# Turning the router's and the experts' operands by DMA instead of by the matrix engine

## What is computed

```
hn = rms_norm(h, ffn_norm_g)                       # per token
group = top1 of 4, experts = top2 of 8 in it       # router: hn @ [w_group_router | w_expert_router], 36 columns
for each 128-row block of rows sorted by expert e:
    a = silu(xb @ w_gate[e]) * (xb @ w_up[e])      # 128 x 512, xb = rows of hn, 128 x 1024
    y = (a @ w_down[e]) * gate                     # added to h at the token's row
```

## Time and profile before

| | us |
|---|---|
| median of 3 runs | 2934.15 (2933.95 to 2938.82) |
| the profiled execution | 2933.64 |
| its span, first to last instruction | 2932.0 |
| PE's first expert matmul | 1513.8 |
| mean granted clock of PE | 0.986 of 2.4 GHz |

### The profile page before, as it was taken

One profiled execution on the slowest core, in us unless ns is written; L12 is line 12 of the kernel. 1 busy time (PEld: TensorE's weight loads), 2 busy tenths in 40 slices (PEclk: granted clock), 3 DMA queues, 4 the chain that ended last, 5 costly groups with the idle time before them and its releaser, 6 DMA issues. The chain is left out here.

```text
span 2932.0 us, 51902 instructions
## 1 busy us (share of the span) xinstructions
PE 2833.6 (97%) x15862; PEld 2015.1 (69%) x15863; DVE 1685.4 (57%) x4102; ACT 1424.0 (49%) x3174; POOL 809.2 (28%) x826
## 2 busy tenths in 40 slices
PE   4999999999999999999859999999999999999998
PEld 2565566556556656655538888888888888888886
DVE  5566666666666666666643546645564545356543
ACT  6655454555455455545423445544454444345433
POOL 1122223313222221321212323323322323333222
PEclk9899999999999999999979999999999999999999
DMA  8112112111211211221335667766776756657763
GB/s 291 40 69 79 57 61 79 66 63 68 79 53 65 79 64 57 75 78 50 140 111 162 183 196 222 237 200 195 233 243 194 229 150 197 180 170 232 241 189 57
DMA packets 152747, 398.52 MB, mean 136 GB/s; under 512 B 18027, under 2 KB 18188, under 8 KB 151692
## 3 DMA queue, kind: packets, MB, share of 16 engines
q1 hardware_dynamic: 123868, 309.36, 30.6%
q0 software_dynamic: 28848, 88.77, 13.0%
HBM read 310.20 MB, written 87.88 MB: 136 GB/s over the span
## 5 line engine op out<-in xcount | busy, mean ns | idle before, releaser
L412 PE MATMUL psG<-wi_all,xT_hi 128*128 128x512 f16 x1024 | 308.1, 383 | 0.7 <-DVE xT_lo L944 0.7
L1333 PE MATMUL psB<-up_hi,gT_hi 128*128 128x512 f32 x632 | 254.2, 402 | 0.0
L1333 PE MATMUL psA<-gate_hi,gT_hi 128*128 128x512 f32 x632 | 246.6, 390 | 3.1 <-ACT gT_hi L1453 1.7
L1333 PE MATMUL psB<-up_hi,gT_lo 128*128 128x512 f32 x632 | 247.4, 391 | 0.0
L1257 POOL DMA_INDIRECT xg<-hn_rows,slots x80 | 98.2, 1228 | 539.7 <-DMA slots<-slot_table 394.2
L1333 PE MATMUL psA<-gate_hi,gT_lo 128*128 128x512 f32 x632 | 246.7, 390 | 0.0
L1333 PE MATMUL psA<-gate_lo,gT_hi 128*128 128x512 f32 x632 | 246.3, 390 | 0.0
L1333 PE MATMUL psB<-up_lo,gT_hi 128*128 128x512 f32 x632 | 246.2, 390 | 0.0
L1469 DVE TENSOR_TENSOR down_lo<-wi_all,down_hi 128x512 fp32r<-128x512 f32 x256 | 157.0, 685 | 147.3 <-ACT down_hi L1427 147.3
L1453 ACT ACTIVATE gT_hi<-psC 128x512 fp32r<-128x512 f32 x80 | 47.8, 598 | 383.1 <-PE psC L1341 383.1
L1483 DVE TENSOR_TENSOR act_rows<-psB,gated 128x512 f32<-128x512 f32 x79 | 54.7, 692 | 289.6 <-PE psB L1333 289.6
(11 more groups left out here) (343 smaller groups left out, 7174.9 us busy)
## 6 DMA issues: line engine op xcount, KB each, us to landing
wi_all<-in_w_gate SPq DMA_DIRECT2D x32, 2048.0 KB, 9.4
wi_all<-in_w_up SPq DMA_DIRECT2D x32, 2048.0 KB, 12.8
wi_all<-in_w_down SPq DMA_DIRECT2D x32, 2048.0 KB, 9.2
xt<-in_x SPq DMA_DIRECT2D x32, 512.0 KB, 3.3
um<-u_rows SPq DMA_DIRECT2D x64, 256.0 KB, 2.7
xres<-in_x SPq DMA_DIRECT2D x32, 512.0 KB, 4.1
out_rows<-h SPq DMA_DIRECT2D x32, 512.0 KB, 2.6
hn_rows<-hn SPq DMA_DIRECT2D x32, 512.0 KB, 2.6
```

What stands on the lines that cost most here:

```text
L412: m = nc.tensor.matmul(ps, left[l][:, k, :], weights.half(r, k, n, width), start=(k == 0 and j == 0), stop=(k == KD - 1 and j == 2))
L1333: m = nc.tensor.matmul(ps[:, :], l[:, k, :], r[:, r_k[n], :], start=(n == 0 and j == 0), stop=(n == len(l_k) - 1 and j == 2))
```

## The change

- Mixer: the f16 halves of `hn` are made while the tokens are still on partitions: the high one by ACT into the buffer `a`, the low one by DVE into `Cs`, both scaled by the router's power of two. SP issues two DMA transposes (`dma_start_transpose`) of 128x1024 f16 into `both_hnT`, and stores the two f16 halves to DRAM in place of the float32 row. PE's transposes of `hn` are gone. PE now runs the router's matmuls after the q projection, and the projection of B last in the body. The load of w_out signals once for all eight pieces.
- Experts: the gathered row holds both f16 halves. ACT's queue issues two DMA transposes of 128x1024 per block (`turn_rows`), ahead of silu. `turn_x` unscales the turned halves in one ACT and one DVE instruction of 128x1024 each.
- The activation stays on its rows. `halve` takes each row's sum of absolute values (ACT), forms a power of two and its inverse (DVE, five one-column steps), makes the f16 halves (ACT, then DVE), and ACT issues two DMA transposes of 128x512. `turn` copies the turned halves. `copy_y` multiplies the gate by the row's inverse on DVE first (`gate_inv`), and ACT waits for that.
- All 12 PE transposes of a block are gone, as is the use of psC, psD and psE there.

```diff
-                after(sp, hn_s, t)
-                sp.dma_start(hn_dram[bass.ds((t - 1) * P, P), :], hn[:]).then_inc(rows_out.sem, 16)
+                after(sp, lg_ps, t - 1)
+                after(sp, hn_hi_s, t)
+                hold(sp, held)
+                sp.dma_start_transpose(both_hnT[:, 0], hn_hi).then_inc(hnT_in.sem, 16)
+                after(sp, hn_lo_s, t)
+                hold(sp, held)
+                sp.dma_start_transpose(both_hnT[:, 1], hn_lo).then_inc(hnT_in.sem, 16)
+                for half, rows in enumerate((a, Cs)):
+                    sp.dma_start(hn_dram[bass.ds((t - 1) * P, P), half * CC:(half + 1) * CC], rows[:]).then_inc(halves_out.sem, 16)
...
+            if full:
...
+                split_mm(psG[:, :], xT, "in", 0, False, range(KD // 2))
...
+                split_mm(psG[:, :], xT, "in", 0, False, range(KD // 2, KD)).then_inc(pq.sem, 1)
             if route:
-                after(pe, hT_dve, t - 1)
+                after(pe, hnT_in, t - 1)
...
-            if attn:
-                after(pe, hn_s, t)
...
-                for b, ps in enumerate((psC, psD)):
-                    for c in range(4):
-                        k = 4 * b + c
-                        m = nc.tensor.transpose(ps[:, c * P:(c + 1) * P], hn[:, k * P:(k + 1) * P], ident)
-                    m.then_inc(hT_ps.sem, 1)
+            if full:
+                after(pe, q_sq, t + 1)
+                after(pe, q_n, t + 1)
+                split_mm(psG[:, :], xT, "in", O_B).then_inc(pb.sem, 1)
...
             if proj:
                 after(act, pc, t + 1)
                 after(act, u_s, t)
+                after(act, hnT_in, t - 1)
+                after(act, halves_out, t - 1)
                 s.activation(Cs[:], psF[:, :], ACT.Copy, scale=inv_in).then_inc(c_sb.sem, 1)
...
+            if attn:
+                after(act, hn_s, t)
+                after(act, mT_ps, t, 1)
+                s.activation(hn_hi, hn[:], ACT.Copy, scale=hn_scale).then_inc(hn_hi_s.sem, 1)
+            if full:
                 after(act, pb, t + 1)
                 after(act, cv, t)
...
                 s.activation(Bs[:], psG[:, :], ACT.Copy, scale=inv_in).then_inc(b_sb.sem, 1)
...
-            if attn:
-                after(act, lg_ps, t - 1)
-                for b, ps in enumerate((psC, psD)):
-                    after(act, hT_ps, t, b + 1)
-                    s.activation(hnT_hi[:, 4 * b:4 * b + 4, :].rearrange("p k c -> p (k c)"), ps[:, :], ACT.Copy,
-                                 scale=hn_scale).then_inc(hT_act.sem, 1)
...
                 after(dve, o_ps, t)
                 after(dve, den_s, t)
                 after(dve, mT_ps, t - 1)
+                after(dve, hnT_in, t - 1)
+                after(dve, halves_out, t - 1)
...
-                after(dve, h_s, t)
-                after(dve, h_rs, t)
-                after(dve, hT_ps, t - 1)
-                v.scalar_tensor_tensor(hn[:], h[:], r_h, g_ffn[:], ALU.mult, ALU.mult).then_inc(hn_s.sem, 1)
...
             if attn:
-                for b, ps in enumerate((psC, psD)):
-                    after(dve, hT_act, t, b + 1)
-                    v.scalar_tensor_tensor(hnT_lo[:, 4 * b:4 * b + 4, :].rearrange("p k c -> p (k c)"), ps[:, :], hn_scale,
-                                           hnT_hi[:, 4 * b:4 * b + 4, :].rearrange("p k c -> p (k c)"),
-                                           ALU.mult, ALU.subtract).then_inc(hT_dve.sem, 1)
+                after(dve, h_s, t)
+                after(dve, h_rs, t)
+                after(dve, hn_hi_s, t - 1)
+                v.scalar_tensor_tensor(hn[:], h[:], r_h, g_ffn[:], ALU.mult, ALU.mult).then_inc(hn_s.sem, 1)
+                if proj:
+                    after(dve, u_s, t + 1)
+                after(dve, hn_hi_s, t)
+                v.scalar_tensor_tensor(hn_lo, hn[:], hn_scale, hn_hi, ALU.mult, ALU.subtract).then_inc(hn_lo_s.sem, 1)
...
+    rows_hi, rows_lo = (xg[:, h * DE:(h + 1) * DE].bitcast(F16) for h in range(2))
+    both_gT16 = wi_flat[:, 3 * 4096:3 * 4096 + KD * P].bitcast(F16).rearrange("p (a k c) -> p a k c", a=2, k=KD)
+    both_aT16 = wi_flat[:, 13312:13312 + DE].bitcast(F16).rearrange("p (a k c) -> p a k c", a=2, k=KE)
+    act16 = wi_flat[:, 13824:13824 + DE].bitcast(F16).rearrange("p (a n) -> p a n", a=2)
+    row_stat, row_bits = sb("row_stat", [P, 8]), sb("row_bits", [P, 2], I32)
+    row_l1, row_scale, row_inv, inv_old, gate_inv = (row_stat[:, n:n + 1] for n in range(5))
...
             if not (isinstance(b, int) and b == 0):
-                pool.wait_ge(xgT_ps, 2 * b)
+                pool.wait_ge(turned, 32 * b)
...
-        def transpose_rows(b):
-            pe.wait_ge(rows_in, 16 * (b + 1))
-            for h, ps in enumerate((psC, psD)):
-                for c in range(4):
-                    m = nc.tensor.transpose(ps[:, c * P:(c + 1) * P], xg[:, (4 * h + c) * P:(4 * h + c + 1) * P], ident)
-                m.then_inc(xgT_ps, 1)
-        def turn_act(b):
-            pe.wait_ge(act_s, b)
-            for c in range(KE):
-                m = nc.tensor.transpose(psE[:, c * P:(c + 1) * P], act_rows[:, c * P:(c + 1) * P], ident)
-            m.then_inc(aT_ps, 1)
...
             if not static0:
-                turn_act(b)
+                pe.wait_ge(act_s, b)
             split_mm(psB, range(KD), (gT_hi, gT_lo), (hi["up"], lo["up"]), list(range(KD)), first, "up", e
                      ).then_inc(up_ps, 1)
-            transpose_rows(b + 1)
...
-    def halves(eng, split, copy_y, act_stage, turn, turn_x):
+    def halves(eng, split, copy_y, act_stage, turn, turn_x, halve, turn_rows=None):
...
                 if not (known and b == 0):
                     eng.wait_ge(up_ps, b)
                 split("up", e)
+            if turn_rows:
+                turn_rows(b + 1)
+                act_stage(b)
             if not (known and b == 0):
                 turn(b)
-            act_stage(b)
+            if not turn_rows:
+                act_stage(b)
             turn_x(b + 1)
+            halve(b)
             if first:
                 if not (known and b == 0):
                     eng.wait_ge(y_ps, 2 * b + 4)
                 split("down", e)
         split("gate", 0)
+        if turn_rows:
+            turn_rows(0)
         turn_x(0)
         total = walk(eng, block_)
         copy_y(total)
         turn(total)
-        copy_y(total + 1)
+        copy_y(total + 1, True)
     gate_of = slots[:, 3, 1:2].bitcast(F32)
...
             for k in range(8):
                 s.activation(hi[n][:, k, :], raw[n][:, k, :], ACT.Copy).then_inc(hi_s[n], 1)
-        def copy_y(b):
+        def copy_y(b, last=False):
             act.wait_ge(y_ps, 2 * b + 1)
             act.wait_ge(shifted, b + 2)
             act.wait_ge(added, 16 * b + 16)
-            s.activation(y[:, 0:512], psF[:, :], ACT.Copy, scale=gate_of).then_inc(y_act, 1)
+            act.wait_ge(gate_s, b + 1)
+            s.activation(y[:, 0:512], psF[:, :], ACT.Copy, scale=gate_inv).then_inc(y_act, 1)
         def silu(b):
             act.wait_ge(gate_ps, b + 1)
...
         def turn(b):
-            act.wait_ge(aT_ps, b)
+            act.wait_ge(aT_in, 32 * b)
             act.wait_ge(y_ps, 2 * b + 2)
-            s.activation(aT_hi[:].rearrange("p k c -> p (k c)"), psE[:, :], ACT.Copy).then_inc(aT_hi_s, 1)
+            s.activation(aT_hi[:], both_aT16[:, 0], ACT.Copy).then_inc(aT_hi_s, 1)
+        def turn_rows(b):
+            act.wait_ge(rows_in, 16 * (b + 1))
+            if not (isinstance(b, int) and b == 0):
+                act.wait_ge(xgT_hi, b)
+                act.wait_ge(xgT_lo, b)
+            for half, rows in enumerate((rows_hi, rows_lo)):
+                hold(act, held)
+                act.dma_start_transpose(both_gT16[:, half], rows).then_inc(turned, 16)
         def turn_x(b):
             if not (isinstance(b, int) and b == 0):
                 act.wait_ge(up_ps, b)
-            for h, ps in enumerate((psC, psD)):
-                act.wait_ge(xgT_ps, 2 * b + h + 1)
-                s.activation(gT_hi[:, 4 * h:4 * h + 4, :].rearrange("p k c -> p (k c)"), ps[:, :],
-                             ACT.Copy).then_inc(xgT_hi, 1)
+            act.wait_ge(turned, 32 * (b + 1))
+            s.activation(gT_hi[:], both_gT16[:, 0], ACT.Copy, scale=inv_hn[:]).then_inc(xgT_hi, 1)
+        def halve(b):
+            act.wait_ge(act_s, b + 1)
+            s.activation(gated[:].bitcast(BF16)[:, 0:DE], act_rows[:], ACT.Abs, accum_out=row_l1).then_inc(l1_s, 1)
+            act.wait_ge(scaled, 5 * b + 5)
+            s.activation(act16[:, 0], act_rows[:], ACT.Copy, scale=row_scale).then_inc(act_hi_s, 1)
+            act.wait_ge(act_hi_s, b + 1)
+            if not (isinstance(b, int) and b == 0):
+                act.wait_ge(aT_lo_s, b)
+            hold(act, held)
+            act.dma_start_transpose(both_aT16[:, 0], act16[:, 0]).then_inc(aT_in, 16)
+            act.wait_ge(act_lo_s, b + 1)
+            hold(act, held)
```

(45 more changed lines are left out.)

89 lines of the change are left out of this document (45 added, 44 removed).

## The result

The changed kernel takes 3587.28 us (median of 4 runs, 3581.32 to 3590.53) against 2934.36 for the kernel before (2933.95 to 2938.82): a ratio of 1.222, 95% interval 1.220 to 1.224. It is 653 us slower. The forecast was 2985, with a range up to 3120. The direction was right and the size was far off.

The account below looks back on a forecast made before the run. PE's list was taken to bound the kernel before, with ACT's list becoming the bound in two-block experts. 2933.6 + 70 (experts) - 28 (mixer) + 9 (ends) = 2985 us, range 2870 to 3120.

Parts of the forecast that it names:

- PE sets the time before, and a steady block or tile has no gap: Both phases: PE, busy 97% of the span, sets the time; expert block 17.72 us, mixer tile 42.96 us.
- The mixer, 28 us in full: Mixer: removing PE's transposes of hn gains 32 x 0.87 = 28 us, taken in full.
- The cover of 14.2 us: Mixer: PE's work from output projection to router's matmuls lasts 14.2 us; the new transpose path needs 11.3.
- the +4 that was forecast: Mixer's last tile: the router's path grows by about 4 us.
- The issue of a transpose, 1.2 us for 128x1024 and half for 128x512: Issuing queue: held 1.2 us per 128x1024 transpose, 0.6 per 128x512; ends 0.35 and 1.65 (0.82).
- The rival built on dear issues: Experts: issues cost 1.65 and 0.82 us, two-block ACT list 41.3, total 3072 us; chance 0.15.
- The landing, 3.3 us after the issue, ends 2 and 6: DMA transposes: data lands 3.3 us after the issue; ends 2 and 6 (half way to a weight load).
- ACT's list, 38.8 us in a two-block expert, 54.0 in a three-block one: Experts: ACT becomes the bound with two blocks, 38.8 against 35.4 us before; three blocks take 54.0 against 53.2.
- the boundary wait: Three-block experts: next gate chunk needs 7.4 us, the down product covers 5.4, so PE waits 2.0 us.
- the forecast had +70: All experts together: +56 us from two-block and +14 from three-block ones, net of PE's saving.
- The clock rival: Experts: stalls lower PE's clock, a third at half speed, over 3300 us; chance 0.13 together with late landing.
- Signs foreseen: Changed profile: PE waits at psA for gate halves and gT_hi, two-block experts 38 to 39 us, ACT's busy share rises.

Follow-up runs that it names:

- e1: Kernel before the change with only the mixer's router part changed (hn by SP's DMA transposes, stored as f32), experts as before: 2911.82 us.
- e11: Changed kernel, but SP issues the weight loads later, behind the landing of the rows' transpose pairs: 3194.51 us.
- after: The changed kernel itself, with the whole change, against the kernel before: 3587.28 us, ratio 1.222.
- e4: Changed kernel without the weight loads of experts 1 to 31 (32 bytes a partition instead), output not the reference's: 3017.62 us, one run.
- e12: e4 with the small tiles row_stat and row_bits allocated behind the other tiles: 3010.83 us, one run.
- e7: Changed kernel, but activation turned by PE as before and the rows' DMA transposes issued by SP a block ahead: 2947.88 us.
- e9: e7 with the small tiles row_stat and row_bits allocated behind the other tiles: 2934.66 us.
- e13: Changed kernel with row_stat and row_bits allocated behind the other tiles and nothing else: 3579.61 us.

## Why the prediction was right or wrong

**PE sets the time before, and a steady block or tile has no gap**: right. 

**The mixer, 28 us in full**: right. 32 x 0.85 = 27 us, and e1 has 23 at the end of the kernel. The cover of 14.2 us held: in the steady tiles PE waited for the transposes once, for 2.8 us. At the last tile the router's matmuls waited 9.6 us for the transposes, where hn and its halves had taken 4.0 + 1.6 before, the +4 that was forecast. The first block came 5.8 us later than in e1 (1495.29 against 1489.52), 3.5 forecast.

**The issue of a transpose, 1.2 us for 128x1024 and half for 128x512**: the first right (1.25), the second not. The activation's took 1.21, median of 79, so half the size cost the same. The prediction's estimate of 1.7 us and half of it, from the Trainium skill's "DMA: Bandwidth & Descriptors", rests on a table that stands in the section "Why a DMA increments its semaphore by 16 and not by 1", not in Bandwidth; the trace has neither the size nor the proportion. The rival built on dear issues did not come: an issue was cheap, or held for several times its upper end of 1.65 us.

**The landing, 3.3 us after the issue, ends 2 and 6**: right without a load in flight. SP's transposes in the mixer landed 3.1 us after the start of their issue, the rows' in e11 3.3 (medians), so about 2.0 after its end. Beside loads it was wrong by far: in after 11.9 us in the median of all 160 and 19.4 at most, outside the ends.

**ACT's list, 38.8 us in a two-block expert, 54.0 in a three-block one**: near in number, but not what sets the time. e4, where only the loads are absent, has 38.86 and 55.90 us. In e4, though, ACT's list is not full. It waits for PE twice in an expert, and PE waits at each boundary (1560 to 2900 us):

```profile
ACT gT_hi L1472 <- PE psB L1352: 116.2, 57, 4.2
ACT down_hi L1436 <- PE psG L1352: 82.5, 29, 2.9
```

```profile
PE psA L1352 <- DVE gate_lo L1501: 102.0, 28, 4.1
```

In one two-block expert of e4, from 2178.10 to 2217.89 us, PE works without a gap for 30.7 us, to the end of the second up product. Then 9.1 us pass until the next gate product can start, and the down product covers 5.6 of them. This is the boundary wait that the forecast had for three-block experts alone, as 7.4 less 5.4 = 2.0 us. It was 3.6 us (median of 31), because from `gT_hi` to the end of the second activation issue it took 5.9 us (2208.81 to 2214.68) and not 4.6, and the registers 1.7 and not 1.3. Behind the wait comes a cost that the forecast had nowhere, PE in order of time:

```profile
2178.10 0.77 PE L1352 MATMUL psA<-gate_hi,gT_hi 128*128 128x512 f32 x1 [3.59 <-DVE gate_lo L1501]
2178.66 0.63 PE L1352 MATMUL psA<-gate_lo,gT_hi 128*128 128x512 f32 x1
2179.09 0.63 PE L1352 MATMUL psA<-gate_hi,gT_lo 128*128 128x512 f32 x1
```

From 2178 to 2182 us the granted clock is 0.50, the lower level, and the first twelve matmuls are about 0.43 us apart. Over the trace the 31 waits are 113 us and the gate products behind them take 53 us longer than the others; against this PE's list is shorter by 79 x 0.92 = 73 (17.72 less 72 x 0.2333 in each block). That is most of the difference: from its first gate product (1492.1) to its end e4 takes 1525.5 us, against 1420.6 before, +105, where the forecast had +70. So the agreement of 38.86 with 38.8 is luck. The sum added up landings that in e4 lie within ACT's waits for PE, and for the two-block expert it had neither the boundary wait nor the clock behind it. Without contention and with matmuls 0.2267 us apart (e12), the forecast of 2985 us is 26 short.

**Where it failed.** The step is the bound on the two unknown costs by the ends of the nearest rows. The upper end of the issue was POOL's scatter, 1.65 us; the second issue of a pair was held for 7.5 or 10.8 us in 60 of 80 pairs. The upper end of the landing was "half way to a weight load", 6 us; it was 11.9 in the median. With the loads gone (e4), 570 of the 653 us are gone. The text had the cause in hand: loads of 2 MB that take 12.8 us, and DMA engines busy for 63%. It priced it as 2.7 us more landing in each block, on the landing alone, and never asked *when* the loads are issued, though its own description of the kernel says it: each as soon as the earlier one is split. It also held the transpose for like the gather, as writing many small pieces; the gather's packets are rows of 4 KB, the transpose's mostly 256 bytes, 1,056 of them an issue. In the rows above, the pair of the first block is issued 0.4 us after gate, with up to follow, and that of the second block 0.2 us after down. The collision is regular, not a matter of chance. And it never asked what ACT does while a second transpose is held: it stands still with silu and `aT_hi` behind it. Both costs have one cause, the packets that are in flight, and the rivals moved them apart. What exactly releases a held issue, no run shows.

**The clock rival** (over 3300 us) was half right. From 2231 to 2245 us, in a down load's collision, PE was busy for 5.48 of 14 us at a granted clock of 0.73:

```profile
2231.00:2245.00 14.00, 5.48 (x20) 4.16 (x19) 2.86 (x6) 1.80 (x3) 2.79 (x5) 0.73 0.85 225
```

The matmuls of the first half of the down product, right after such a wait, are 0.413 us apart in the median of 79 blocks, against 0.2334 in e4. PE's matmuls of the experts can be added up in both traces. From the first to the last they take 2075.9 us in after and 1510.9 in e4. Of the 565 us between, 426 are waits and 139 are longer distances between the same matmuls, 126 of these in the first half of the down product, behind the waits for `aT_hi`. The mean granted clock in this part is 0.85 in after and 0.95 in e4. So about a quarter of the loss is matmuls at the lower clock behind the waits. No run changes the clock alone.

**Signs foreseen**: PE at psA waiting for the gate halves came (100.8 us). Waits for `gT_hi` at psA did not, since PE stood at psF for `aT_hi` first (431.5 us). ACT's busy share fell where it was to rise: it was busy for 115 us more, in a span that grew by 652, and its issues don't count as busy.

## What to carry to other kernels

Here a DMA of many small packets took turns by number with the loads beside it. So price such a DMA beside the transfers that are in flight at that moment, and look up when these are issued: a landing of 3 us became 12 in the median and 19 at most. Issue it from an engine with nothing urgent behind it, a whole block ahead, since the issue itself can be held, here for up to 12.5 us. Before a change removes PE's work, ask which engine takes over its timing: the router's transposes went into 14 us of cover and were gained in full, the experts' went into a list that hands on at each expert's boundary and had no cover there. And there, after waits of 3.6 us (e4), PE ran on at the lower clock, which cost another 1.7 us in the mean.

## What the runs showed of the hardware

A transpose of 128x512 f16 is issued in 1.21 us and one of 128x1024 in 1.25: nearly a fixed cost. The last packet of two row transposes, 0.5 MB, starts 4.0 us after the first issue if no load is in flight, 12.3 us after it beside one load of 2 MB in 4 KB packets, and 18.5 beside two loads in 2 KB packets (medians). Where both queues have packets, they leave one for one by number (e.g. 814 against 819 in 5 us).

Two tiles, 40 bytes a partition together, ahead of PE's operands in the allocation made the experts' 128x512 matmuls 3% slower (0.2333 us apart instead of 0.2267 at a granted clock of 1.00), and moving them behind undid it (e7 and e9, e4 and e12, after and e13). Which of the tiles behind them has to lie how was not tried.
